# Expert stage of a hybrid encoder step: 32-row blocks in four column tiles, fp32 weights passed unsplit

## What is computed

```python
D_MODEL, SEQ, DEC_BATCH, DEC_SEQ, PAST_LEN = 1024, 512, 8, 16, 256
N_HEADS, QK_HEAD_DIM, V_HEAD_DIM, N_EXPERTS, D_EXPERT = 8, 64, 128, 16, 512

def _diff_scores(qb, k, v, lam, mask):          # sample tokens: 256 cached and the new keys
    s = jnp.einsum('bqhmd,bkhmd->bmhqk', qb, k).astype(jnp.float32) * scale
    ...
    p = jax.nn.softmax(s, axis=-1)
    w = p[:, 0] - lam * p[:, 1]
    return jnp.einsum('bhqk,bkhd->bqhd', w, v.astype(jnp.float32))
...
attn = _rmsnorm(attn, lp['subln_g']) * (1.0 - lam_init)      # per head, over V_HEAD_DIM
...
def _hier_moe(xn, lp):                          # g_sel: best group; top_i: two experts in it
    ...
    for e in range(N_EXPERTS):
        h = jax.nn.silu(xt @ lp['w1'][e]) * (xt @ lp['w3'][e])
        y = y + combine[:, e:e + 1] * (h @ lp['w2'][e]).astype(f32)
    return y.astype(xn.dtype).reshape(shp)
```

## Time and profile before

| | us |
|---|---|
| median of 3 runs | 1378.24 (1377.75 to 1378.33) |
| profiled execution | 1380.1 |
| its span, first to last instruction | 1378.3 |
| attention stage | 527 |
| merge stage | 253 |
| output projection and routing | 115 |
| expert stage | 432 |
| end | 31 |
| mean granted TensorE clock | 0.94 |

### The profile page before, as it was taken

The page is one execution under the profiler, slowest core; times in us unless marked ns, Lnnn a source line. Parts: engine busy times, 40 slices in busy tenths (PEclk is TensorE's granted clock), DMA queues, the critical chain, the costliest instruction groups (busy, mean ns, idle before and its releaser), DMA issues. The chain is left out here.

```text
span 1378.3 us, 20707 instructions
## 1 busy us (share of the span) xinstructions
PE 1194.5 (87%) x7034; PEld 1034.6 (75%) x7035; DVE 795.4 (58%) x1184; ACT 544.6 (40%) x873; POOL 507.9 (37%) x267
## 2 busy tenths in 40 slices
PE   2899999999899997899899999848888989988980
PEld 1797989899898985799899955536677768766760
DVE  5335767575666757800322112266888988888865
ACT  2123342323334143311200001216677868767752
POOL 4434251514325110566646600013443444444432
PEclk9999999999999997899999999858999999999995
DMA  4352151332415100322432168004997583799946
GB/s 163 88 155 65 53 157 57 106 101 62 116 47 161 44 27 28 118 77 72 154 117 76 50 239 328 31 31 153 326 356 264 183 297 116 281 342 353 354 160 243
DMA packets 185410, 211.90 MB, mean 154 GB/s; under 512 B 12599, under 2 KB 131383, under 8 KB 185350
## 3 DMA queue, kind: packets, MB, share of 16 engines
q1 hardware_dynamic: 176422, 178.56, 39.0%
q0 software_dynamic: 4608, 16.78, 3.4%
q10 hardware_dynamic: 4320, 15.73, 2.9%
HBM read 184.50 MB, written 26.36 MB: 153 GB/s over the span
## 5 line engine op out<-in xcount | busy, mean ns | idle before, releaser
L1775 ACT ACTIVATE ch<-w 128x1024 fp32r<-128x1024 f32 x240 | 252.3, 1060 | 117.8 <-PE bank L1715 95.9
L1839 DVE TENSOR_TENSOR cl<-w,ch 128x1024 fp32r<-128x1024 f32 x180 | 261.0, 1497 | 41.2 <-ACT ch L1775 36.5
L1685 POOL TENSOR_TENSOR cl<-w,ch 128x1024 fp32r<-128x1024 f32 x60 | 154.2, 2570 | 228.8 <-ACT ch L1775 228.8
L171 POOL TENSOR_TENSOR wh<-raw,zcol 128x1024 fp32r<-128x1024 f32 x40 | 77.6, 1940 | 298.6 <-DMA raw<-in_w_in 240.4
L1713 PE MATMUL bank<-ch,xeh 128*128 128x512 f32 x320 | 133.0, 416 | 45.5 <-DVE cl L1839 42.4
L1715 PE MATMUL bank<-ch,xel 128*128 128x512 f32 x320 | 127.1, 397 | 0.0
L1714 PE MATMUL bank<-cl,xeh 128*128 128x512 f32 x320 | 127.0, 397 | 0.0
L593 PE MATMUL bank<-xh,wh 128*128 128x320 f32 x384 | 122.5, 319 | 0.0
L594 PE MATMUL bank<-xl,wh 128*128 128x320 f32 x384 | 119.3, 311 | 0.0
L595 PE MATMUL bank<-xh,wl 128*128 128x320 f32 x384 | 119.2, 310 | 0.0
L1713 PEld LDWEIGHTS bank<-ch,xeh 128*128 128x128 f32 x320 | 61.4, 192 | 71.6 <-DVE cl L1839 55.4
(11 more groups left out here) (286 smaller groups left out, 2717.1 us busy)
## 6 DMA issues: line engine op xcount, KB each, us to landing
w<-in_w SPq DMA_DIRECT2D x64, 1024.0 KB, 15.0
w<-in_w SPq DMA_DIRECT2D x16, 2048.0 KB, 9.7
raw<-in_w_in SPq DMA_DIRECT2D x40, 512.0 KB, 4.7
block_outputs<-yb ACTq DMA_DIRECT2D x21, 512.0 KB, 7.3
kc<-in_cache_k SPq DMA_DIRECT2D x8, 1024.0 KB, 6.6
vc<-in_cache_v SPq DMA_DIRECT2D x8, 1024.0 KB, 5.3
...
```

The lines of the kernel that those rows point to most:

```text
L1685: nc.gpsimd.tensor_tensor(cl[:, c % RING5, :, :], S.raw(c), ch[:, c % RING5, :, :].bitcast(F32), ALU.subtract).then_inc(ch_low_pool, 1)
L1775: nc.scalar.activation(ch[:, c % RING5, :, :], S.raw(c), ACT.Copy).then_inc(ch_high, 1)
L1839: nc.vector.tensor_tensor(cl[:, c % RING5, :, :], S.raw(c), ch[:, c % RING5, :, :].bitcast(F32), ALU.subtract).then_inc(ch_low_dve, 1)
```

## The change

- `G` = 4, `B` = 32: blocks have 32 rows. `OVMAX` becomes 39, `NBLK` 55; the routing loops run to `OVPER` = 19.
- TensorE's expert products are unsplit fp32. The block's 32 rows are stationary (128*32) and the weights move; the four groups of 128 hidden (or 256 output) columns go to four partition ranges of one bank, `bank[2][B * j:B * (j + 1)]`. `ch`, `cl` and all splitting of the stage are gone. Hidden values lie as 128 partitions (4 groups x 32 rows) by 128, so one transpose turns them.
- Tokens: `xg` is 32 rows; of the 8 transposes the first covers 128 partitions (`xrows`, rows 32 to 127 set to zero), the others 32.
- Weights: ten units `wbuf` of 2 MB; an expert takes three (first and second half of up, down). Six are loaded in the stage before, as the two experts were. `release` waits for the last block that used a unit.
- Experts are written out instead of looped in pairs; further blocks of an expert stay an inner loop.
- Results of a block are copied by VectorE alone and stored by four DMAs of 32 x 256.
- Sample values: the weights are stationary (`wTp`, zero padded to 32 columns for a pair of streams, and `wTn` for the new keys), the cached values move, 128 columns. The result has queries as rows, goes into `oraw` as a fifth tile and is normed with the prompt's tiles. `oTs` and its norm in the merge stage are gone; ten groups of four transposes replace eight.

```diff
...
+G = 4
+B = P // G
+OVMAX = (NSEL - NE) // B
+OVPER = TOK // B - 1
 NBLK = NE + OVMAX
 NROWS = NBLK + 3
...
-        wTs = sb("wTs", [P, 3, P], ctx=st2)
+        wTn = wT[1][:, 0:P]
+        wTp = sb("wTp", [P, NS, 4 * DS], ctx=st2)
...
-                            mm = nc.tensor.matmul(bank[7][:, b * DS:(b + 1) * DS], vc[:, 2 * b + k, :],
-                                                  wTs[:, k, b * DS:(b + 1) * DS], start=False,
-                                                  stop=True, skip_group_check=True)
+                    nc.tensor.matmul(bank[7][:, 0:P], wTn, kvt[:, 1 + par, NQ, :], start=True, stop=True)
+                    for k in range(2):
+                        for odd in range(2):
+                            for j in range(NS // 2):
+                                mm = nc.tensor.matmul(bank[7][2 * DS * j:2 * DS * (j + 1), 0:P],
+                                                      wTp[:, k * 4 + j, 2 * DS * odd:2 * DS * (odd + 1)],
+                                                      vc[:, 2 * (2 * j + odd) + k, :], start=False,
+                                                      stop=True, skip_group_check=True)
...
+                def sample_weights(S):
+
+                    act.wait_ge(pt_done, S.h * NT + 5)
+                    tb = bank[5 + (S.par * NT + 4) % 2]
+                    for odd in range(2):
+                        nc.scalar.activation(wTp[:, :, 3 * DS * odd:3 * DS * odd + DS],
+                                             tb[:, 0:2 * P].rearrange("p (n c) -> p n c", c=2 * DS)
+                                             [:, :, DS * odd:DS * (odd + 1)], ACT.Copy)
+                    nc.scalar.activation(wTn, tb[:, 2 * P:3 * P], ACT.Copy).then_inc(pt_out, 1)
...
-                    turned(S, 4, wTs[:, :, :].rearrange("p k q -> p (k q)"), 3 * P)
+                    sample_weights(S)
...
-                    nc.vector.tensor_scalar(oTs[:, bass.ds(h, 1), :], bank[7][:, 0:P]
-                                            .rearrange("p (o c) -> p o c", o=1), 1.0, None, ALU.mult) \
-                        .then_inc(os_out, 1)
+                    nc.vector.tensor_copy(oraw[:, par * NO, :], bank[7][:, 0:P]).then_inc(os_out, 1)
...
-            for g in range(2):
-                pe.wait_ge(osq_ready, g + 1)
-                nc.tensor.matmul(bank[g][:, :], ones, roots3[g][:, 0:512], start=True, stop=True) \
-                    .then_inc(oms_done, 1)
-            for h in range(H):
...
+            for u in range(NTURN):
+                if u >= 4:
+                    pe.wait_ge(at_low, u - 3)
+                if u == H - 1:
                     pe.wait_ge(rnn_done, H)
-                for t in range(NQ):
-                    mm = nc.tensor.transpose(bank[4 + h % 4][:, t * P:(t + 1) * P], on[:, h, t, :], ident)
+                for a in range(4):
+                    h, t = (u, a) if u < H else (4 * (u - H) + a, NQ)
+                    tile = on[:, h, t if h % 2 else (t + 1) % NO, :]
+                    mm = nc.tensor.transpose(bank[4 + u % 4][:, a * P:(a + 1) * P], tile, ident)
                 mm.then_inc(at_done, 1)
-            pe.wait_ge(oroot, 2)
...
+            norm_attention(dve, tail_chain, H - 1, 1)
+            for u in range(NTURN):
+                dve.wait_ge(at_high, u + 1)
+                nc.vector.scalar_tensor_tensor(turned_out(bl, u), turned_bank(u), subln[:, 0:1],
+                                               turned_out(bh, u).bitcast(F32), ALU.mult, ALU.subtract) \
+                    .then_inc(at_low, 1)
...
+    UNITS, UNIT = 3, 2 * (KT // 2) * FE
+    FIRST, WBUFS = 6, 10
+    wbuf = [sb(f"wbuf{i}", [P, UNIT]) for i in range(FIRST)]
...
-            ts(ov, cnt, float(P), None, ALU.is_gt)
-            for j in range(2, TT):
-                chain(nc.vector.scalar_tensor_tensor(ov, cnt, float(j * P), ov, ALU.is_gt, ALU.add))
+            ts(ov, cnt, float(B), None, ALU.is_gt)
+            for j in range(2, OVPER + 1):
+                chain(nc.vector.scalar_tensor_tensor(ov, cnt, float(j * B), ov, ALU.is_gt, ALU.add))
...
-            ts(q, rank, float(P), None, ALU.is_ge)
-            for j in range(2, TT):
-                chain(nc.vector.scalar_tensor_tensor(q, rank, float(j * P), q, ALU.is_ge, ALU.add))
-            chain(nc.vector.scalar_tensor_tensor(place, q, -float(P), rank, ALU.mult, ALU.add))
+            ts(q, rank, float(B), None, ALU.is_ge)
+            for j in range(2, OVPER + 1):
...
     def each_block(eng, step, last):
-
-        def count(row, e, top_):
-            return eng.value_load(row[0:1, bass.ds(e, 1)], min_val=0, max_val=top_)
-
-        def expert(e, up, down):
-            if down is None:
-                step(Turn(0, up, None))
-            else:
-                step(Turn(count(ovp, e, OVMAX) + e, up, down))
-            n = count(ovc, e, TT - 1)
+        for e in range(NE):
+            step(Turn(count(eng, ovp, e, OVMAX) + e if e else 0, e, e - 1 if e else None))
+            n = count(eng, ovc, e, OVPER)
             with eng.If(n > 0):
-                with eng.Fori(count(ovp, e, OVMAX - 1), count(ovp, e + 1, OVMAX)) as j:
-                    step(Turn(j + (e + 1), up, up))
-
-        expert(0, (0, 1), None)
-        with eng.Fori(0, NE // 2 - 1) as i:
-            expert(i * 2 + 1, (1, i + 1), (0, i + 1))
-            expert(i * 2 + 2, (0, i + 2), (1, i + 1))
-        expert(NE - 1, (1, NE // 2), (0, NE // 2))
-        last(Turn(count(ovp, NE, OVMAX) + NE, None, (1, NE // 2)))
+                with eng.Fori(count(eng, ovp, e, OVMAX - 1), count(eng, ovp, e + 1, OVMAX)) as j:
+                    step(Turn(j + (e + 1), e, e))
+        last(Turn(count(eng, ovp, NE, OVMAX) + NE, None, NE - 1))
...
+            def last_block(e):
+
+                return count(sp_, ovp, e + 1, OVMAX) + e
+
+            def release(e, u):
+
+                n = UNITS * e + u - WBUFS
+                if n >= 0:
+                    sp_.wait_ge((up_half, up_all, down_all)[n % UNITS], last_block(n // UNITS) + 1)
+
+            for e in range(2, NE):
+                for half in range(2):
+                    release(e, half)
+                    load_up(sp_, e, half)
+                release(e, 2)
+                load_down(sp_, e)
...
             def step(S):
-                for c in range(RING5 - 1, UPC if S.down is None else NCH, RING5):
-                    low(S, c)
                 gather(S.b + 2)
...
+            def up(S):
+                pe.wait_ge(xt_ready, S.b + 1)
+                for half in range(2):
+                    if half and S.down is not None:
+                        turn_hidden()
+                    arrived(pe, S.up, half)
+                    w = up_weights(S.up, half)
+                    for k in range(KT // 2):
+                        t = half * KT // 2 + k
+                        for j in range(G):
+                            mm = nc.tensor.matmul(bank[2][B * j:B * (j + 1), 0:2 * FG].rearrange("p (i f) -> p i f", i=2),
+                                                  xT[:, t * B:(t + 1) * B], w[:, :, k, FG * j:FG * (j + 1)],
+                                                  start=(t == 0), stop=(t == KT - 1))
+                    mm.then_inc((up_half, up_all)[half], 1)
 
             def turn_tokens(b):
                 pe.wait_ge(xg_in, b * 16 + 16)
-                if not isinstance(b, int) or b > 0:
-                    pe.wait_ge(xt_high, b)
-                    pe.wait_ge(xt_low, b)
-                for k in range(KT):
-                    mm = nc.tensor.transpose(bank[k // 4][:, k % 4 * P:(k % 4 + 1) * P], xg[:, k * P:(k + 1) * P],
-                                             ident)
+                nc.tensor.transpose(bank[0][:, 0:P], xrows[:, 0:P], ident)
+                for k in range(1, KT):
+                    mm = nc.tensor.transpose(bank[0][:, k * B:(k + 1) * B], xg[:, k * P:(k + 1) * P], ident[0:B, 0:B])
                 mm.then_inc(xt_done, 1)
 
             def turn_hidden():
-                for k in range(DNC):
-                    mm = nc.tensor.transpose(bank[4][:, k * P:(k + 1) * P], gg[:, k * P:(k + 1) * P], ident)
+                for i in range(HC):
+                    mm = nc.tensor.transpose(bank[4][:, i * P:(i + 1) * P], gg[:, i * P:(i + 1) * P], ident)
                 mm.then_inc(ht_done, 1)
...
             def down(S):
 
-                pe.wait_ge(y_act, S.b)
-                pe.wait_ge(y_dve, S.b)
-                pe.wait_ge(ht_high, S.b)
-                pe.wait_ge(ht_low, S.b)
-                for c in range(UPC, NCH):
-                    chunk(S, c)
+                pe.wait_ge(ht_ready, S.b)
+                pe.wait_ge(y_ready, S.b)
+                arrived(pe, S.down, 2)
+                w = down_weights(S.down)
+                for c in range(FE // P):
+                    s = c % HC * P + c // HC * B
+                    for j in range(G):
+                        mm = nc.tensor.matmul(bank[5][B * j:B * (j + 1), 0:DG], hT[:, s:s + B],
```

(31 more changed lines are left out.)

356 lines of the change are left out of this document (105 added, 251 removed).

## The result

The changed kernel takes **1330.34 us** (median of 4 runs, 1324.61 to 1331.9) where the kernel before, on the same chip, takes 1378.28: ratio 0.964, 95% interval 0.961 to 0.967. The profiled execution is 1331.58 us with a span of 1329.5, 48.8 less than before's 1378.3. The prediction was 1277: the sign held and the time lies in the range, but less than half of the forecast gain came.

A forecast was written before the change was run, and what follows sets the result against it. TensorE was taken to bound attention, with four engines nearly level in the expert stage. Experts -69.7, sample values -32.2, merge -6.1 and +6.5 for routing and a memset took 1380.1 to 1278.6, median 1277 us; range 1250 to 1338 (82%).

The forecast's parts named there:

- The step: Expert stage, TensorE's work per 32-row block: 6.8 us, from products 5.12, transposes 0.89 and changes of shape 0.8.
- Rivals B: Expert stage: column tiles don't keep four in flight, 62.5 ns a record for 53.3, +0.9 us a step, 1309; 7%.
- D: Expert stage: column tiles go one after another, 15 us more a step, over 1800 us; under 1%.
- The sum for experts 0 to 7: Expert stage: TensorE sets the pace, 36 steps taking 244.8 us, 255.4 us until the first unit is freed.
- Rival A: Expert stage: the gather into single buffer xg becomes the step's bound, 1300 to 1338 us; 20%.
- rival C: Expert stage: TensorE's clock falls; at 1.2 GHz throughout, step 12.8 us, time 1495; 8%, a smaller share 5%.
- Experts 8 to 15: Late expert stage: the weight stream sets the pace, 38.3 MB at 395 GB/s, 96.9 us, after 1.5 us until transfers flow.
- The tail: Expert stage after the last weights: down 3.4 us, copy 0.5, four issues 1.4, landing and gate 2.9.
- Sample values: Attention heads: shorter product group and no low-clock stretch behind it, 4.6 us a head over seven heads, -32.2 us.
- 0.5 us exposed if not: Attention heads: VectorE's norm over five tiles instead of four costs 0.5 us a head, expected hidden.
- Merge: Merge stage: sample rows' sums of squares, roots, reciprocals and late splits go, -6.1 us.
- routing: Routing stage: two loops over multiples of 32 need 30 more chained VectorE instructions at 0.2 us, +6.0 us.

The follow-up runs named there:

- t_thin: Changed kernel with every weight load from the eleventh unit on cut to a quarter of its bytes, so later experts compute with partly old weights: 1277.82 us.
- x_ahead: Changed kernel with gathers one block further ahead, landing in a second buffer that GpSimd copies to the rows TensorE reads: 1495.99 us, ratio 1.087.
- l_loop: Changed kernel with expert 0 written out, experts 1 to 15 as five looped rounds of three, and nine weight units for ten: 1324.16 us, ratio 0.960.
- w_nine: Changed kernel with nine weight units in place of ten and nothing else: 1331.13 us, ratio 0.965.

## Why the prediction was right or wrong

**The step: right.** Forecast 6.8, measured 6.52; four tiles in flight, 5.46 us for 96 records. The total is closer than its parts: the products took 0.34 more than the 5.12 forecast, the transposes and changes of shape 1.06 where 1.69 was forecast. Rivals B (62.5 ns a record, measured 57) and D fall. By the 2.38 times of the Trainium skill, page TensorE: Matmul & The Clock Gate (Part 3, Measured speedup vs the span model), that the prediction weighed, the products would take 6.5 us; they took 5.5, so this trace does not show that loss with four tiles of 256 moving columns.

**The sum for experts 0 to 7: wrong, and this is the step that failed.** Forecast 255.4 us from the first index copy to the free first unit of expert 7; measured 285.4 (SyncE's next load is issued at 1175.65). Of the +30.0, the eight first steps of experts carry +29.8 (84.2 us for 8 x 6.8), the other 28 steps -3.0, start and half an up +3.2. I took one step time for all 36 and no price for a change of expert. Rival A had the wait with the right landing (up to 6.9, a step up to 9.15), but in every step, where it came in the first ones alone, and without the code. I gave it 20%, with the argument that a gather of a quarter of the bytes lands 1 us earlier, so 3.1 to 5.9. Measured: 2.8 with the stream at rest, 6.7 with it running. The landing times in the earlier trace rows were a mixture, and I subtracted bytes from it where the stream was the cause: a change that frees weight buffers in bursts makes the late kind the rule exactly where an expert begins. Reading the landing by stretches of DMA load would have pointed the right way, but not far enough: in the kernel before it is 4.4 us (median) in 1060 to 1160 at 178 GB/s and 5.4 in 1202 to 1326 at 340 GB/s. 6.7 for a quarter of the bytes stands in no row of it.

**Code: not seen at all.** "Experts written out" is in the change and I costed it at nothing. With the register loads it is 1.2 us a first step and 1.6 to 3.7 a single-block expert beside light traffic (t_thin), more beside the full stream (single waits up to 3.9 us, 2.7 in t_thin). No row that I quoted could show it; the page's instruction queue, 42 packets for a looped program, could have raised the question.

**The clock, rival C: in part.** Mean 0.92 in the stage for 0.97 before. Not from narrow tiles alone: in the steps inside experts 5 and 7 it is 1.00. Where it falls, a wait stands ahead (0.76 behind that of expert 5; 0.72 to 0.85 throughout in x_ahead), but not each wait brings it down: behind the 2.5 to 2.9 us of experts 1 to 4 it stays at 1.00, and what makes the difference is open. It costs 0.7 us in expert 5's first step and in expert 6's about the 1.7 by which that step is longer than in experts 1 to 4. From expert 8 on it is 0.73 to 0.88 over six of the nine steps; no run prices that.

**Experts 8 to 15: 98.4 forecast, some 111 measured** (1175.65 to the last landing near 1287, from SyncE's last issue at 1272.6 and the median of 14.8 us). The rate of the running stream was 383 GB/s where 395 was forecast, and 351 over the whole stretch (windows of the changed kernel, columns as above):
```profile
1240.00:1260.00 20.00, 12.82 (x162) 6.42 (x166) 1.95 (x7) 0.66 (x2) 1.05 (x2) 0.83 1.05 383
```
since it nearly stood still once: expert 8's first step waited 4.8 us for rows and ran at the low clock, and so freed the next unit late:
```profile
1190.00:1195.00 5.00, 5.00 (x56) 2.30 (x59) 0.57 (x2) 0.38 (x1) 1.05 (x2) 0.55 0.12 39
```
That the stream alone ends these experts, as I forecast, is not shown: in the changed kernel TensorE names no wait for weights (20.3 us in l_loop), stops for 19.2 us in seven waits for nothing named from 1222 to 1290, and a unit more in w_nine cost nothing. Here the two end nearly level.

**The tail: 8.2 forecast, about 11.** The last two blocks share `yb`, so the second copy waits 2.70 us for the first one's four stores.

**Sample values: mechanism right, size too large.** The group takes 1.08 us for 3.7 to 4.5, and the 0.50 stretches behind it are mostly gone: attention's clock 0.98 for 0.94. From the start of the first head's group to that of the last it is -23.6 us (87.1 to 511.3 before, 87.8 to 488.4 after), 3.4 a head for 4.6. What I called hidden ("0.5 us exposed if not") was 1.0 us a head: TensorE waits for VectorE's `ebuf`, 22.6 us in 21 waits for 13.2 in 15. One of them, from PE's time line:
```profile
208.49 0.33 PE L641 MATMUL bank<-cst,ebuf 128*128 128x128 f32 x1 [1.00 <-DVE ebuf L899]
```
The last group is 2.9 shorter too, and that comes back in the last head, where VectorE sets the end anyway (one wait of 7.0 us, before 4.3). **Merge** -7.5 for -6.1; **routing** +5.4 for +6.0 (TensorE's wait for the table 13.0 us, before 6.9): both right.
